# A softmax with its score factor folded into the queries' norm weights, its maximum written negated, and its scaling done with one scalar per partition

## The reference

```
q = axial_rope(rmsnorm(q, q_g), ang_row, ang_col)     # 8 query heads of 64
k = axial_rope(rmsnorm(k, k_g), ang_row, ang_col)     # 2 key heads of 64
scale = HEAD_DIM ** -0.5                              # 0.125
def block(qblk):                                      # 128 queries
    s = einsum('bqkgd,bskd->bkgqs', qblk, k) * scale  # against all 1024 keys
    p = softmax(s, axis=-1)
    return einsum('bkgqs,bskd->bqkgd', p, v)
```

## Time and profile before

| what | value |
|---|---|
| median of 3 runs | 2309.35 us (2302.63 to 2311.84) |
| profiled execution, first to last instruction (span) | 2307.9 us |
| time of the profiled execution around its span | not recorded; the median is 1.45 us above the span |
| PE busy | 96% of the span |
| DVE, ACT, POOL busy | 70%, 47%, 34% |
| mean granted clock of PE | 0.989 of full speed |
| the 64 units of the second attention | from 1357 us to about 1557 us of the span |

### The profile page before, as it was taken

The page is one execution under the profiler, slowest core; times in us unless marked ns, Lnnn a source line. Parts: engine busy times, 40 slices in busy tenths (PEclk is TensorE's granted clock), DMA queues, the critical chain, the costliest instruction groups (busy, mean ns, idle before and its releaser), DMA issues. The chain is left out here.

```text
span 2307.9 us, 29073 instructions
## 1 busy us (share of the span) xinstructions
PE 2218.0 (96%) x10136; PEld 1787.9 (77%) x10136; DVE 1617.7 (70%) x2247; ACT 1089.5 (47%) x1877; POOL 795.6 (34%) x579
## 2 busy tenths in 40 slices
PE   6999998999899999999998999999999999999998
PEld 4778887686678888888876767767778888887887
DVE  6468447626999999985797379994575555556686
ACT  5232256735644444455445368882343333334533
POOL 1030024513533232342023626661274444433310
PEclk9999999999999999999999999999999999999999
DMA  9156622033133333289944230003422333339986
GB/s 348 56 174 212 203 85 64 26 128 115 45 111 101 105 101 110 81 296 394 335 165 139 72 101 19 23 5 110 145 69 98 107 101 106 101 119 320 354 277 228
DMA packets 282565, 331.82 MB, mean 144 GB/s; under 512 B 18281, under 2 KB 180409, under 8 KB 282049
## 3 DMA queue, kind: packets, MB, share of 16 engines
q1 hardware_dynamic: 279760, 322.57, 41.4%
q0 software_dynamic: 2208, 7.37, 0.9%
q10 hardware_dynamic: 465, 0.17, 0.0%
HBM read 251.11 MB, written 78.94 MB: 143 GB/s over the span
## 5 line engine op out<-in xcount | busy, mean ns | idle before, releaser
L2643 PE MATMUL ps<-sum_hi,whi 128*128 128x512 f32 x640 | 249.5, 390 | 1.0 <-DVE wlo L2809 0.7
L2645 PE MATMUL ps<-sum_hi,wlo 128*128 128x512 f32 x640 | 249.0, 389 | 0.0
L2644 PE MATMUL ps<-sum_lo,whi 128*128 128x512 f32 x640 | 249.0, 389 | 0.0
L2669 PE MATMUL ps<-sum_lo,whi 128*128 128x512 f32 x616 | 240.7, 391 | 2.0 <-ACT arena L2754 2.0
L2671 PE MATMUL ps<-sum_lo,wlo 128*128 128x512 f32 x616 | 239.7, 389 | 0.0
L2670 PE MATMUL ps<-sum_lo,whi 128*128 128x512 f32 x616 | 239.7, 389 | 0.0
L2643 PE MATMUL ps<-hhi,whi 128*128 128x512 f32 x480 | 188.3, 392 | 9.0 <-DVE cbuf L3324 3.3
L226 DVE TENSOR_TENSOR wlo<-raw,whi 128x1024 fp32r<-128x1024 f32 x56 | 78.4, 1406 | 159.6 <-ACT whi L221 159.5
L2644 PE MATMUL ps<-hlo,whi 128*128 128x512 f32 x480 | 188.2, 392 | 0.0
L2645 PE MATMUL ps<-hhi,wlo 128*128 128x512 f32 x480 | 188.0, 392 | 0.0
L1732 POOL TENSOR_TENSOR cbuf<-cbuf,attn_stats 128x1024 f32<-128x1024 f32 x80 | 151.5, 1894 | 94.0 <-DVE attn_stats L1993 94.0
(11 more groups left out here) (450 smaller groups left out, 5575.2 us busy)
## 6 DMA issues: line engine op xcount, KB each, us to landing
shared<-ffn_blocks SPq DMA_DIRECT2D x154, 256.0 KB, 5.1
lead_work<-in_w_down SPq DMA_DIRECT2D x105, 256.0 KB, 4.4
arena<-in_w_down SPq DMA_DIRECT2D x100, 256.0 KB, 4.1
raw<-in_w_up SPq DMA_DIRECT2D x36, 512.0 KB, 5.1
ffn_blocks<-chunk_work SPq DMA_DIRECT2D x66, 256.0 KB, 2.3
ffn_blocks<-lead_work SPq DMA_DIRECT2D x66, 256.0 KB, 2.3
raw<-in_w_in SPq DMA_DIRECT2D x32, 512.0 KB, 4.7
arena<-in_w_ada SPq DMA_DIRECT2D x32, 512.0 KB, 5.5
```

What stands on the lines that cost most here:

```text
L2643: nc.tensor.matmul(o, hi[:, ws], mhi, start=fresh and k == 0, stop=False, skip_group_check=True)
L2644: nc.tensor.matmul(o, hi[:, ws], mlo, start=False, stop=False, skip_group_check=True)
L2645: mm = nc.tensor.matmul(o, lo[:, ws], mhi, start=False, stop=(k == 3), skip_group_check=True)
L2669: nc.tensor.matmul(o, hi[:, ws], mhi, start=fresh, stop=False, skip_group_check=True)
```

## The change

Four edits. (1) At the program's start DVE multiplies `qg` by SC, 0.125, once. The scores of the second attention then come out multiplied already, and ACT's exponential has no scale. (2) In the second attention the reduce writes the negated maximum itself, straight into the place of `ng`, and the small multiplication behind it, with its wait for the reduce, is gone. (3) POOL's multiplication there is a TENSOR_SCALAR with a scalar per partition read from `st` instead of a TENSOR_TENSOR whose second operand is the same column broadcast over 1024 elements. (4) POOL's instructions for the second attention are written out for all 8 blocks instead of in the loop. The first attention keeps scale, multiplication and loop.

```
+                ch.step(nc.vector.tensor_scalar(qg, qg, SC, None, ALU.mult))
                 nc.vector.tensor_scalar(sinks, sinks_in, -1.0, None, ALU.mult).then_inc(sinks_scaled, 1)
...
-                            q = 1 if full else 4
-                            p = prob[sl].rearrange("p (r k) -> p r k", k=T // q)
-                            nc.gpsimd.tensor_tensor(p, p, st[:, sl, 16:16 + q].unsqueeze(2).to_broadcast([P, q, T // q]),
-                                                    ALU.mult).then_inc(S["scaled"], 1)
+                            if full:
+                                nc.gpsimd.tensor_scalar(prob[sl], prob[sl], st[:, sl, 16:17], None, ALU.mult)\
+                                  .then_inc(S["scaled"], 1)
+                            else:
+                                p = prob[sl].rearrange("p (r k) -> p r k", k=wk)
+                                nc.gpsimd.tensor_tensor(p, p, st[:, sl, 16:20].unsqueeze(2).to_broadcast([P, 4, wk]),
+                                                        ALU.mult).then_inc(S["scaled"], 1)
...
-                    query_blocks(pool, ahead, body)
                     if full:
+                        ahead()
+                        for i in range(NB):
+                            body(At(i), i + 1 < NB)
                         lead.pool_last(pool)
                         following.pool(pool)
+                    else:
+                        query_blocks(pool, ahead, body)
...
-                            nc.scalar.activation(prob[sl], up[sl][:, :], ACT.Exp, scale=SC, bias=st[:, sl, 4:5],
+                            nc.scalar.activation(prob[sl], up[sl][:, :], ACT.Exp, bias=st[:, sl, 4:5],
...
-                        nc.vector.tensor_reduce(mx, up[sl].rearrange("p (r k) -> p r k", k=wk), AX.X, ALU.max)\
-                          .then_inc(S["stat"], 1)
-                        dve.wait_ge(S["stat"], u.val(add=1))
                         if full:
-                            nc.vector.tensor_scalar(ng, mx, -SC, None, ALU.mult).then_inc(S["neg_max"], 1)
+                            nc.vector.tensor_reduce(ng, up[sl].rearrange("p (r k) -> p r k", k=wk), AX.X, ALU.max,
+                                                    negate=True).then_inc(S["neg_max"], 1)
                         else:
+                            nc.vector.tensor_reduce(mx, up[sl].rearrange("p (r k) -> p r k", k=wk), AX.X, ALU.max)\
+                              .then_inc(S["stat"], 1)
+                            dve.wait_ge(S["stat"], u.val(add=1))
```

## The result

The changed kernel takes 2328.29 us (median of 4 runs, 2322.87 to 2331.97) against 2308.3 us of the kernel before (also 4 runs): a ratio of 1.0095, 95% interval 1.0076 to 1.0113. It is slower by 0.95%, and the forecast was 2303.7 us with a range up to 2311. The span of its profiled execution is 2330.2 us, 22.3 us more than the span in the earlier trace rows.

A forecast was written before the change was run, and what follows sets the result against it. The prediction took a chain over ACT and DVE, with PE waiting inside it, to set the 11.85 us group; 3.0 + 0.3 + 1.5 + 0.8 = 5.6 us gained gave 2303.7 us, range 2296 to 2311.

The forecast's parts named there:

- POOL's multiplication: POOL's scaling in the second attention: from 1.894 us to 1.05, gaining only at the start (1.5 us) and end (0.8 us).
- In the steady group nothing: Second attention's steady groups: POOL's 0.85 us less buys nothing by itself, only lets DVE's 0.17 us count.
- Rival C: POOL's scaling by a column is slow and decides beyond about 2.0 us: 5 us more at 2.40, 22 at 3; chance 0.07.
- The small multiplication (DVE): Second attention, reduce to subtraction: 1.34 us falls to 1.12 to 1.23, a group to 11.60; 3.0 us plus 0.3 outside.
- The sum: Whole kernel: 3.0 + 0.3 + 1.5 + 0.8 = 5.6 us gained, giving a span of 2302.3 us and a time of 2303.7.
- DVE's term: Second attention, reduce to subtraction: gain of 0.17 us, the middle of 0.11 to 0.22, which made the sum 4.4 to 6.6.
- The chain over `copy_out`: Closing of a group of four units: a path over ACT and DVE of 6.27 us, falling to 6.10, with PE waiting inside.
- Alone, neither edit would give much there.: Steady group: subtraction and POOL's scaling release the transposes nearly together, so DVE's or POOL's edit by itself gives little.
- The factor in qg: One more DVE instruction of about 0.17 us at 41.7 us, hidden by 0.40 us of cover; exponential without scale costs 0.
- the written-out loop: POOL's 64 multiplications written out: counted as 0, with slack of 1.1 us a unit to cover fetching more code.
- The end: Behind the second attention: PE has no longer gap but a 12.27 us DMA that moves along, so the gain reaches the end.

The follow-up runs named there:

- the constant in two operations: Changed kernel with GpSimd multiplying by constant 1 and adding constant 0, the division by the row sums left out: 2301.26 us, ratio 0.9976.
- the run with only the fast form: Kernel before with only GpSimd changed: scalar from a column plus a constant 0, its loop written out: 2306.0 us, ratio 0.9999.
- the longer scaling: Changed kernel with GpSimd multiplying by a tile of ones as full second operand, the division left out: 2312.62 us, ratio 1.0030.

## Why the prediction was wrong

The step that failed is "POOL's multiplication": "So the new one costs between 1.03 and 2.40. I take 1.05: it reads one tile as the first row does, and the column is one element per partition." It costs 2.85. The value was wrong, and so was the upper bound; the two bounds came from rows that differ from the new form in more than the one thing that I weighed. The row at 1.03 differs in the scalar (a constant) and in the number of operations (two). I discussed the first, which costs 0.07 us, and did not see the second, which costs 1.7. In the sum the step shows where it says "In the steady group nothing": with 2.85 us the scaling stands in both rings, and a group takes 13.28 us instead of 11.60.

- *The rival that happened.* Rival C had the mechanism, and its starting point, 2.0 us, lies between the two that the traces give: about 1.8 in the closing ring, 2.2 in the other. At 2.40 it priced a group at 12.2; 12.36 came at 2.39. It had a chance of 0.07, because its price at 2.85 lay outside the bounds that I had set. Its own table was nearly right: 22 us at 3 us of duration, where 20 came of 2.85.
- *The small multiplication (DVE).* Right in its mechanism. From reduce to subtraction 1.14 us came (expected 1.12 to 1.23). The group with the scaling of 1.05 us is 11.50, expected 11.60; the 11.62 with TENSOR_TENSOR is nearer, but by another path, since POOL holds the closing turn there. The reduce with negated output is as long as the plain one, 1.22. The subtraction started 0.08 us before the reduce's recorded end, as the reciprocal's row had shown. The section that the prediction cites, "The DRAIN you can't avoid" in "VectorE: DVE Perf Modes" of the Trainium skill, goes on to say that a next operation that is not held starts earlier, which the prediction left out; the row agrees with that.
- *The sum.* With the duration that I assumed, the constant in two operations gives ratio 0.9976, and 2303.7 / 2309.35 is 0.9976. Part of that is luck. In the traces the stretch from the first scaling to the last turn became 6.4 us shorter, not 5.6: 4.2 in the 12 groups (forecast 3.0), 2.2 outside them (forecast 2.6). The groups were forecast too long because PE's own time for a unit is 2.72 us there, not the 2.75 read from block 0, and the closing turn and the one behind it take 6.06 us together, where 6.10 was forecast for the chain. Outside, the third turn still waited 0.47 us, now for DVE, so the 0.39 there did not simply go. And DVE's term stands 17 times in the sum, so that 0.11 or 0.22 makes it about 4.6 or 6.5, not 4.4 or 6.6. The chain over `copy_out` that held the gain down was real: taking it apart gave another 0.27 us a group.
- *"Alone, neither edit would give much there."* Half right. POOL's edit alone gives nothing (11.85 a group). DVE's alone gives 0.23 of the 0.35 us: 0.12 in the two turns that do not wait for POOL (5.56 to 5.44), and 0.11 in the closing turn and the one behind it (6.29 to 6.18). There PE still waits for POOL, and only a shorter scaling brings the other 0.12.
- *The factor in qg, the written-out loop.* No price found, as forecast: the run with only the fast form has the loop written out and a group of 11.85, as before. The factor was not run by itself; the versions that have it are among the fastest, which leaves room for the 0.17 us that it would cost without cover.
- *The end.* What the second attention lost reached the kernel's end: 22.1 of 22.3 us.

What stays open is why GpSimd runs one operation slower than two. That the ring goes over ACT's order and not only over the two `prob` tiles is read from the timeline: the turn at 1447.49 is over at 1448.58, and the exponential starts at 1449.15, when ACT is done with the copies. A third tile or another order on ACT was not tried.

## What to carry to other kernels

A price borrowed from another row holds only if the row has the same form: engine, operation, number of operations, kinds of operands. List every difference before using it, and where one is left, keep a cost of a multiple of the nearest row as a real case and not as a tail (here it was 2.7 times the row taken). An engine that is idle a fifth of the time can still set the pace, if its duration stands whole in a ring over several engines. Add up each such ring by itself (here over two units, which is also the number of buffers), and its sum tells at which duration the engine begins to count there; a mean over different rings does not. On GpSimd, in float32 and at 512 to 2048 elements as measured here, write a multiplication by a scalar as multiply and add 0.

## What the runs showed of the hardware

- GpSimd's TENSOR_SCALAR on 128x1024 float32, alone: 2.77 to 2.85 us with one operation, 1.05 to 1.12 with two; TENSOR_TENSOR 1.89 with a broadcast column and 2.34 with a full tile.
- VectorE's reduce with negated output over 1024 elements takes 1.22 us, as the plain one does.
- VectorE's subtraction of two tiles in SBUF (query low part, 1024 elements), started while GpSimd was scaling, took 1.90 us beside TENSOR_TENSOR and 1.33 beside the slow TENSOR_SCALAR. First the kernel before, then the changed kernel:

```profile
1361.60 1.90 POOL L1732 TENSOR_TENSOR cbuf<-cbuf,attn_stats 128x1024 f32<-128x1024 f32 x1 [4.82 <-DVE attn_stats L1993]
...
1362.68 1.90 DVE L3802 TENSOR_TENSOR arena<-arena,cbuf 128x1024 fp32r<-128x1024 f32 x1
```
```profile
1361.00 5.73 POOL L1732 TENSOR_SCALAR cbuf<-cbuf,attn_stats 128x1024 f32<-128x1024 f32 x2 [4.67 <-DVE attn_stats L2002]
...
1361.86 1.33 DVE L3811 TENSOR_TENSOR arena<-arena,cbuf 128x1024 fp32r<-128x1024 f32 x1
```

Beside TENSOR_TENSOR the subtraction ends 1.08 us behind GpSimd's instruction (1364.58 against 1363.50). It does so too where TENSOR_TENSOR was put back (2.08 us long, 1.08 behind) and with the longer scaling (2.55 us long, 1.09 behind), as if it did its work only once GpSimd was done. Beside the one-operation TENSOR_SCALAR it ends while GpSimd's first scaling still runs (1363.19 against 1363.86), and in the run with only GpSimd changed likewise (1.22 us long). The slow form disturbs VectorE less. The two-operation form does not have that advantage: in the trace of the kernel before, L3579 on GpSimd ends at 1277.59, and a subtraction on VectorE (L226) that started at 1277.09 beside it took 1.57 us instead of 1.22 and ended 1.07 behind.
